# A hybrid mLSTM and Fourier layer on one core: new order of the front loads, earlier staging of the branch tiles, and the first layer norm folded into the feed-forward product

## What is computed

```
mod = silu(c) @ w_mod + b_mod                 # 1024 -> 6*1024: sh1, sc1, g1, sh2, sc2, g2
h = x * (1 + sc1) + sh1
q, k, v, o, gates, uf, ga, gb = split(h @ w_in)
y_a = (norm(mlstm(q, k, v, gates)) * sigmoid(o)) @ w_branch_a   # 4 heads, two directions
y_b = fourier(uf) @ w_branch_b
out = (sigmoid(ga) * y_a + sigmoid(gb) * y_b) @ w_out
x1 = layer_norm(ALPHA * x + g1 * out) * ln_gain[0] + ln_bias[0]
h2 = x1 * (1 + sc2) + sh2
a, u = split(h2 @ w_ffn_in)                   # 1024 -> 2 * 2816
x2 = layer_norm(ALPHA * x1 + g2 * ((silu(a) * u) @ w_ffn_out)) * ln_gain[1] + ln_bias[1]
```

## Time and profile before

| | us |
|---|---|
| median of 3 runs | 1601.06 (1599.74 to 1605.26) |
| profiled execution | 1602.63 |
| its span | 1600.8 |
| TensorE busy | 1484.3 (93%) |
| VectorE, ScalarE, GpSimd busy | 690.5, 323.6, 807.3 |
| mean granted clock of TensorE | 0.96 |
| DMA | 160.75 MB, mean 100 GB/s |

### The profile page before, as it was taken

How to read it: one execution, slowest core, us unless ns; L and a number is a source line. 1 busy time by engine, 2 the same in 40 slices (tenths; PEclk the granted TensorE clock), 3 DMA queues, 4 the chain that set the end, 5 groups by cost and what they waited for, 6 DMA issues and landing times.

```text
span 1600.8 us, 24150 instructions
## 1 busy us (share of the span) xinstructions
PE 1484.3 (93%) x9737; PEld 1440.2 (90%) x9737; DVE 690.5 (43%) x1066; ACT 323.6 (20%) x496; POOL 807.3 (50%) x365
## 2 busy tenths in 40 slices
PE   5899998999999999999987998875999999999994
PEld 4798898989989989989987998875999999999994
DVE  5522388725724734743624674456333111101114
ACT  1222311122122122122223000224122212100002
POOL 2172256663354254254235675446666666656552
PEclk7799999999999999999998999996999999999997
DMA  8121135521221231142135443121332222242221
GB/s 348 64 67 38 61 114 191 192 77 59 93 92 61 89 107 53 57 134 73 40 132 177 150 154 144 40 66 79 119 105 105 77 67 79 79 151 73 72 72 66
DMA packets 56230, 160.75 MB, mean 100 GB/s; under 512 B 5960, under 2 KB 20560, under 8 KB 54872
## 3 DMA queue, kind: packets, MB, share of 16 engines
q1 hardware_dynamic: 39608, 146.78, 26.3%
q10 hardware_dynamic: 16544, 12.82, 2.5%
HBM read 142.24 MB, written 17.33 MB: 100 GB/s over the span
## 4 chain that ended last, share of the span: by engine, by line
PE 82%; DVE 9%; issue 3%; POOL 2%; ACT 2%; DMA 2%; SPq 0%; ACTq 0%; DVEq 0%; POOLq 0%
PE psum L703 63%; PE psum L959 7%; PE psum L943 4%; PE psum L777 2%; PE psum L899 1%; DMA raw<-in_wunits 1%; DVE prod_z L1425 1%; PE psum L752 1%; PE psum L728 1%; PE psum L862 1%; PE psum L1018 1%; POOL w_lo L615 1%; POOL r_all L675 1%; DVE rows L1866 0%; DVE prod_f L1453 0%
## 5 line engine op out<-in xcount | busy, mean ns | idle before, releaser
L611 POOL TENSOR_TENSOR w_hi<-raw,zero 128x1024 fp32r<-128x1024 f32 x156 | 299.2, 1918 | 610.5 <-PE psum L703 519.7
L615 POOL TENSOR_TENSOR w_lo<-raw,w_hi 128x1024 fp32r<-128x1024 f32 x164 | 421.3, 2569 | 67.1 <-ACT w_hi L1128 54.9
L703 PE MATMUL psum<-h_hi,w_hi 128*128 128x256 f32 x1600 | 374.7, 316 | 48.9 <-DVE h_lo L1409 30.3
L703 PE MATMUL psum<-h_lo,w_hi 128*128 128x256 f32 x1600 | 372.2, 314 | 0.0
L703 PE MATMUL psum<-h_hi,w_lo 128*128 128x256 f32 x1600 | 371.1, 314 | 0.0
L703 PEld LDWEIGHTS psum<-h_hi,w_hi 128*128 128x128 f32 x1600 | 296.1, 193 | 51.8 <-issue 37.2
L703 PEld LDWEIGHTS psum<-h_lo,w_hi 128*128 128x128 f32 x1600 | 299.0, 193 | 0.0
L703 PEld LDWEIGHTS psum<-h_hi,w_lo 128*128 128x128 f32 x1600 | 298.7, 193 | 0.0
L1821 DVE TENSOR_TENSOR ff_sb<-psum,s_sb 128x640 f32<-128x640 f32 x22 | 18.2, 825 | 160.5 <-PE psum L703 148.6
L703 PE MATMUL psum<-f_hi,w_hi 128*128 128x256 f32 x352 | 81.4, 313 | 2.8 <-DVE f_lo L1409 2.8
L703 PE MATMUL psum<-f_lo,w_hi 128*128 128x256 f32 x352 | 80.9, 311 | 0.0
(11 more groups left out here) (276 smaller groups left out, 2510.8 us busy)
## 6 DMA issues: line engine op xcount, KB each, us to landing
raw<-in_wunits SPq DMA_DIRECT2D x164, 512.0 KB, 3.3
mod_first<-in_wmod SPq DMA_DIRECT2D x16, 512.0 KB, 15.5
z_ring<-in_wmod SPq DMA_DIRECT2D x16, 512.0 KB, 3.9
yg_dram<-yg_sb ACTq DMA_DIRECT2D x20, 256.0 KB, 2.6
yg_st<-yg_dram SPq DMA_DIRECT2D x16, 320.0 KB, 3.6
c_raw<-in_stateC SPq DMA_DIRECT2D x4, 1028.0 KB, 5.9
mod_ring<-in_wmod SPq DMA_DIRECT2D x8, 512.0 KB, 3.5
mod_late<-in_wmod SPq DMA_DIRECT2D x8, 512.0 KB, 4.4
```

What stands on the lines that cost most here:

```text
L611: pool.tensor_tensor(hi, src, zero[:, 0:1].broadcast_to([P, src.shape[1]]), ALU.add)\
L615: pool.tensor_tensor(lo, src, hi.bitcast(F32), ALU.subtract).then_inc(w_split, 1)
L703: ins = mm(out[:, a:z], w[:, slot, cols], x[:, k, a:z], start=(start and n == 0), stop=(stop and n == 2))
```

## The change

1. *Front.* SP loads `c_rows` straight into `silu_z` first, and ScalarE applies Silu to it (two operations of 128 x 1024). The diagonal products, the four broadcast matmuls and their copies go. The loads of S (sh1) stand ahead of C (sc1) tile by tile, those of tile 1 ahead of the weights. Scale tiles are computed two ahead. ScalarE modulates both token groups.
2. *Modulation.* `z_ring` has six slots and the loads 0 to 5 are issued at once. The last 8 tiles move from the feed-forward to the branch product (`MIX_MODS`), two per output tile throughout. `c_raw` of a head also waits for `mod_sum1` >= 24.
3. *Branch tiles.* `yg_hi` and `yg_lo` are laid out anew so that the tiles of heads 0 and 1 can be staged during the last head, those of head 2 beside gate unit 5 and those of head 3 behind it; the wait for the state stores and the load of the silu rows go behind the first weights of the branch product.
4. *Output product.* The first two units run 7 blocks each (`leading`), then the last block of each (`closing`). The totals `sum_1` and `sum_2` are kept by VectorE, and `column_sums` is once two fp32 products with ones.
5. *Norm.* The feed-forward product takes g = h2_s * r (r is the residual, not normed) and, as columns 640 to 643, the columns h2_s and h2_b for both groups (`aug`). With W the weights, rstd * (W g - mu * W h2_s) + W h2_b is W h2. So each eviction copies the four columns (`w4`), adds nmu * w4, multiplies by rstd, and takes the bias in the Silu or in the gated product. x1 is made in the first 8 pairs, on VectorE and ScalarE. GpSimd only splits weights.

The core of the diff ("..." marks what is left out):

```diff
-Z_LOADS = (0, 2, 2, 3, 5, 7, 10, 13, 16)
+ZR = 6
+Z_LOADS = (0, ZR, ZR, ZR, 7, 9, 11, 14, 16)
-MIX_MODS = (16, 18, 20, 22, 24, 24, 24, 24, 24)
+MIX_MODS = (16, 18, 20, 22, 24, 26, 28, 30, 32)
+NA = 4
+NX = NT + NA
...
+            def z_mod_unit(n):
+                if n >= ZR:
+                    sp.wait_ge(mod_sum1, KD + n - ZR + 1)
+                sp.dma_start(z_ring[:, n % ZR, :], wmod2[n]).then_inc(mod_in[n], 16)
...
+            sp.dma_start(silu_z[:], c_rows).then_inc(row_in, 16)
+            first_mod(S[0], C[0])
             sp.dma_start(bmod_sb[:], bmod).then_inc(bmod_in, 16)
-            first_mod(C[0], S[0])
             x_part(0)
+            first_mod(S[1], C[1])
             weights(0)
-            first_mod(C[1], S[1])
             weights(1)
...
                     if r == 3:
                         sp.wait_ge(c_ok, h + 1)
+                        sp.wait_ge(mod_sum1, 3 * KD)
...
+            weights_next(U_GA + 2)
+            sp.wait_ge(yg_stored, 16 * (2 * TT + 1))
+            sp.wait_ge(num_done, H * TT)
+            yg_head(0)
+            weights_next(U_GA + 3)
+            weights_next(U_GA + 4)
+            yg_head(1)
+            weights_next(U_GA + 5)
+            sp.wait_ge(yg_stored, 16 * (3 * TT + 1))
+            yg_head(2)
+            weights_next(U_GA + 6)
+            sp.wait_ge(yg_stored, 16 * (H * TT + 1))
+            yg_head(3)
+            weights_next(U_GA + 7)
...
+            def leading(out, u, slot, act_hi, act_lo, ready, given, end=NT):
+                pe.wait_ge(w_split, u + 1)
+                for b in range(UB - 1):
+                    pe.wait_ge(ready, given + b + 1)
+                    block(out, slot, b, act_hi, act_lo, b, b == 0, False, end)
+            def closing(out, slot, act_hi, act_lo, ready, given, end=NT):
+                pe.wait_ge(ready, given + UB)
+                block(out, slot, UB - 1, act_hi, act_lo, UB - 1, False, True, end).then_inc(units_done, 1)
...
             scale_tile(0)
+            scale_tile(1)
...
-                if b + 1 < KD:
-                    scale_tile(b + 1)
+                if b + 2 < KD:
+                    scale_tile(b + 2)
...
+            def column_sums():
+                for out, total, done in ((joined(2), sum_1, s1_ok), (joined(3), sum_2, s2_ok)):
+                    pe.wait_ge(done, KD + 1)
+                    for a, z in ((0, CUT), (CUT, NT)):
+                        ins = mm(out[:, a:z], ones_r[:].bitcast(F32), total[:, a:z], start=True, stop=True)
+                ins.then_inc(stats_done, 1)
             for p in range(2):
                 pe.wait_ge(taken[p], A_OUT + 1)
+                leading(joined(p), U_OUT + p, p, mg_hi, mg_lo, m_ok, 2)
+            for p in range(2):
+                closing(joined(p), p, mg_hi, mg_lo, m_ok, 2)
...
+            leading(joined_x(0), U_FF1, 0, g_hi, g_lo, g_ok, 2, NX)
+            column_sums()
+            pe.wait_ge(taken[1], A_FF1 + 1)
+            leading(joined_x(1), U_FF1 + 1, 1, g_hi, g_lo, g_ok, 2, NX)
             for p in range(2):
+                closing(joined_x(p), p, g_hi, g_lo, g_ok, 2, NX)
...
                 gated(h, 3)
                 if not last:
                     qk_rest(h + 1, 2)
+                else:
+                    yg_rest(0)
                 gated(h, 4)
                 odd_state(h, 1, 5)
                 if not last:
                     qk_rest(h + 1, 3)
+                else:
+                    yg_rest(1)
                 odd_state(h, 3, 7)
...
+            v.wait_ge(yg_stored, 16 * (H * TT + 1))
+            for r in range(KV):
+                v.wait_ge(st_stored[r], 16 * (H + 1))
+            yg_rest(2)
+            yg_rest(3)
...
+            def normed(i, p, t, done):
+                v.wait_ge(units_done, U_FF1 + 2 * i + p + 1)
+                v.tensor_copy(w4[:, p, :], joined_x(p)[:, NT:NX]).then_inc(w4_ok, 1)
+                v.wait_ge(w4_ok, 2 * i + p + 1)
+                for g, span in enumerate(halves):
+                    ins = v.scalar_tensor_tensor(out=t[:, span], in0=nmu[:, span], scalar=w4[:, p, g:g + 1],
+                                                 in1=joined(p)[:, span], op0=ALU.mult, op1=ALU.add)
+                ins.then_inc(taken[p], 1)
+                v.wait_ge(taken[p], A_FF1 + i + 2)
+                v.tensor_tensor(t[:], t[:], rstd_b[:], ALU.mult).then_inc(done, 1)
             def gated_unit(i):
+                normed(i, 0, ta, ta_ok)
+                normed(i, 1, tb, tb_ok)
+                v.wait_ge(tb_ok, i + 1)
+                v.wait_ge(s_ok, i + 1)
+                for g, span in enumerate(halves):
+                    ins = v.scalar_tensor_tensor(out=ff_sb[:, span], in0=tb[:, span], scalar=w4[:, 1, 2 + g:3 + g],
+                                                 in1=s_sb[:, span], op0=ALU.add, op1=ALU.mult)
+                ins.then_inc(ff_ok, 1)
                 v.wait_ge(f_hi_ok, i + 1)
                 sub(f_lo[:, i, :], ff_sb[:], f_hi[:, i, :]).then_inc(f_ok, 1)
```

376 lines of the change are left out of this document (176 added, 200 removed).

## The result

The changed kernel takes 1535.06 us in the median of four runs (1533.22 to 1542.28), the kernel before 1600.51 beside it (1599.74 to 1605.26): a ratio of 0.9586, 95% interval 0.9549 to 0.9623. The forecast was 1527 in a range of 1510 to 1550: the sign and the range hold, the size is 8 us too hopeful. The profiled execution took 1533.22 us (span 1531.4).

A forecast was written before the change was run, and what follows sets the result against it. TensorE, busy for 93% of the span, was taken as the bound. Gains 16 + 6 + 13 + 45 less losses 1 and 5 make 74; 1602.6 - 74 = 1528.6, less 1.6: 1527 us, range 1510 to 1550.

The forecast's parts named there:

- Front: Start to end of the eighth block: earlier start and cheaper tiles move its end from 75.12 to 59, gain 16 us.
- I take half of its steps at each clock: end at 59: Front loop: half its steps at 1.2 GHz and half at 2.4 GHz, between ends of about 68 and 50.
- Rival 1: Front runs at 2.4 GHz with vector-bound tiles, ending at 50, 9 us better: 1518 us; chance 12%.
- Branch-b stage: Six ring slots remove TensorE's 4.29 us wait for weights and one half-clock stretch (1.7): gain 6 us.
- Last head and gates: Branch product starts at 863 instead of 874.54, with a 4.5 us wait before gate unit 7 left: gain 13 us.
- Output product and first norm: Last branch unit to third feed-forward unit falls from 126.2 to 81.6 us: gain 45.
- They end last: Before the third feed-forward unit: the weight split ends at +20 and rules, after the statistics at +18.5.
- Feed-forward: Four extra columns cost 1.9 us over 42 units, entered as loss 1; VectorE's added work inside the pairs costs nothing.
- rival 3: VectorE, waiting for GpSimd, becomes the feed-forward's bound: up to 8.8 us more per pair, 1712 us; chance 8%.
- Last pair: End of feed-forward: a chain of 5.5 to 8 us against 2.84, plus 1.7 for the clock: loss 5.
- 2: Rival: branch-tile copies delay the last gating, gate unit 7 or first branch unit stays late: 1543 us; chance 10%.
- 4: Rival: the fold does nothing, TensorE still waits for the statistics; 17 us return, 1553 with a late front; chance 2%.

The follow-up runs named there:

- e6: Changed kernel with TensorE's wait for the last feed-forward tile moved from ahead of the output product to ahead of its third unit; median 1532.67 us.
- e4: Changed kernel with the last gate unit's weights issued on SP ahead of the last four branch tiles instead of behind them; median 1542.15 us.
- e3: Changed kernel with the modulation ring back to two buffers and its loads in the earlier kernel's order; median 1539.07 us.
- e10: Changed kernel with e2b, e4, e5, e6, the first two units' weights earlier and one branch-b modulation unit reduced in a VectorE gap; median 1516.75 us.
- e5: Changed kernel with the scaling of the residual input on ScalarE instead of VectorE; median 1533.32 us.
- e13: Changed kernel with TensorE making the column sums, then waiting for rstd_b before its first feed-forward block; median 1560.57 us.
- e2b: Changed kernel with the first norm's output spread over 12 feed-forward pairs instead of 8, its store one pair later than in a first try; median 1540.77 us.
- e9: Changed kernel with 14 extra fp32 matmuls where TensorE idles at the start, before the first real block; median 1541.29 us.
- e11: Changed kernel with each eighth of the gate product inside the front's loop, behind its tile's block, and scale tiles behind the block; median 1542.68 us.
- e12: e10 with the gate product of the first three tiles inside the front's loop, the other five eighths behind the last block; median 1512.76 us.

## Why the prediction was right, and where it was off

The forecast of 1527 held by its range, and its nearness is in part luck. Every term but the front's and the last pair's came out worse than forecast, and the early clock in the front covered for them. With the late clock of e6 or e4 (11.1 or 15.6 us more) the profiled execution would have been at 1544 to 1549, an estimate, and still inside 1550.

**Front, 16 predicted, 22.8 in the profile.** The start (25 predicted, 26.42) and the two ends came out near: 50 at 2.4 GHz, 68 at 1.2 GHz; measured 52.13, and 67.72 in e4. The start is late because the second split takes 6.1 us, not 4.3 to 4.5, beside VectorE's reductions. The step that failed is "I take half of its steps at each clock: end at 59". No profiled execution did that: they have the clock up at about 30 us (five with the changed kernel's front: gate product at 52.1 to 53.0) or not until 56 to 66 (three: 63.2, 67.4 and 67.7). Rival 1, at 12%, is what the profiled execution did in the front, though not its 1518 for the whole. A mean of two modes was put in the place of two cases with a chance each; that 1542.28, the highest of the changed kernel's runs, had the late clock fits, but only profiled runs show it. Also wrong was the pace: VectorE's 3.7 us per tile were to bind, but it needs some 3.4 and waits 0.16 for TensorE, whose 3.55 bind.

**Branch-b stage, 6 predicted, 2.5 in the profile, 2.7 by e3.** The wait went as said. The step that failed is "the wait goes, and one half-clock stretch with it", with nothing said of what is late next. With the ring no longer in the way VectorE works without a break to 285 us (busy for 34.0 of the 35 us from 250), and the unit at 286.42 waits 2.59 us for `q_lo`. The earlier trace rows gave 1.5 us for a reduction; beside GpSimd's work the 32 of this stage take 2.1 in the mean (busy us in all, mean ns):

```profile
L1471 DVE CUSTOM_DVE_ANT_0 prod_z<-z_ring,silu_z,bmod_sb 128x1024 f32<-128x1024 f32 x32 | 67.6, 2114 | 2.0
```

e10 shows the other side: one unit moved into a gap of VectorE, and the wait is gone.

**Last head and gates, 13 predicted, 11.5.** The wait of 4.5 us for gate unit 7 is there with 4.61, for the cause named. e4 shows that it was avoidable, and that it costs 7.1.

**Output product and first norm, 45 predicted, 42.** From the end of the last branch unit (952.1) to the third feed-forward unit 84.3 us, 81.6 predicted. Both waits for GpSimd are longer than the 3.5 expected: 5.61 and 4.25. The mis-sized term is the split, "4.3": at the first place it is 6.3, since VectorE's long scaling runs beside it (e5), at the second 4.9. "They end last" was right: statistics at 1031.9, split at 1036.4. e13 bears out that hiding them is worth 16 of the 42 us.

**Feed-forward, -1 predicted, -4.2.** The columns cost 0.04 us a unit, as the prediction worked out. The sum entered 1 where its own sentence works out 1.9. "Even 11 us stay inside a pair: nothing" failed: VectorE is busy for 13.5 to 13.6 us of 14.7 to 14.8 in a steady pair of the first eight. Two operations that were put at 1.6 together take 2.5 and 2.9 there, and the product with `rstd_b`, put at 0.8, takes up to 2.5 (timeline of one pair):

```profile
1081.20 2.46 DVE L1869 TENSOR_TENSOR ta<-ta,rstd_b 128x640 f32<-128x640 f32 x1
...
1089.42 2.52 DVE L1886 TENSOR_TENSOR r_all<-r_all,nmu 128x640 f32 x1
1091.98 2.90 DVE L1888 TENSOR_TENSOR r_all<-r_all,rstd_b 128x640 f32 x1
```

This is rival 3's mechanism at up to 0.7 us per pair (14.83 against 14.16), in eight pairs only; 3.5 us more in every pair were needed to turn the sign. By the prediction's own signs of being wrong (TensorE waiting for VectorE inside the product, units over 7.3 us) these eight pairs are it: six waits for `ta`, units of 7.4 us. e2b has it back in part.

**Last pair, -5 predicted, -4.7.** 7.56 us idle in 5.5 to 8; e6 shows that the whole of it was a wait put further forward than its reader needs.

**Rivals.** 2 did not happen: from the last wait for `kw_f` to gate unit 4, a stretch that holds the last head, 124.2 us pass before and after, so the copies in it moved nothing. 4 is refuted by e13.

## To carry to other kernels

A wait should stand ahead of the first instruction that reads the data, and a weight load ahead of everything in its queue that it does not need: the two cheapest edits here (e4, e6) gave 7.1 and 9.6 us in their stretches, more than the waits they removed, because the half-clock stretch behind each went too. When a transfer stops being the limit, add up the busy time of the engine behind it, at the durations that it has beside GpSimd's work and not at the quiet ones, before taking the wait as a gain. And where a stretch may run at either clock, give the two cases a chance each; the runs of e9 and e10 suggest that one kernel can be both from one execution to the next.

## What the runs showed of the hardware

One and the same front, with TensorE busy from 26.5 us on without a gap, worked at the durations of the full clock from 30 us on in five profiles and from 56 to 66 in three. The Trainium skill (TensorE: Matmul & The Clock Gate, Part 1, "The two states") has a sustained busy TensorE at 2.4 GHz; these three executions speak against that for a loop of which half the time goes to matmuls of two columns. The row of the granted clock does not show it: in e4's window below it reads 1.00, while scale tiles take 3.41 us. In the kernel before the same window reads 0.68. So the late clock is read from durations, which are those of 1.2 GHz elsewhere (3.54 and 0.73 us), and no run shows why the row disagrees with them.

```profile
30.00:60.00 30.00, 30.00 (x131) 30.00 (x130) 14.05 (x26) 8.69 (x13) 2.35 (x1) 1.00 0.32 122
```

With the block ahead of its scale tile and gate matmuls behind (e11, e12) ten runs of two kernels stayed within 5.0 and 4.4 us; extra work only ahead of the loop (e9) left a spread of 19. If each execution were late with the three chances in eight of the profiles, ten early ones in a row would come about once in a hundred times, an estimate; that the eight unprofiled ones were early is read from the spread alone. What decides between the two in a given execution stays open.

GpSimd's subtraction of 1024 columns took 2.35 us beside ScalarE's scaling and 4.14 beside VectorE's.
